# Two forget tables in two PSUM banks, ahead of the values' compression

## The chip, the cores and the metric

The kernel runs on one core of one Trainium2 chip. The metric is the device time of one execution in microseconds (us); lower is better. The kernel is one program of some 22,700 instructions in which the order on every engine is written out by hand and engines meet only at counting semaphores.

## What is computed

The program computes two transformer blocks on 512 tokens of width 1024, in float32. The change lies wholly in the first block, between its input projections and its first attention:

```python
log_f = jax.nn.log_sigmoid(f_f + b_forget).transpose(0, 2, 1)      # (B, H=8, S=512)
# fox_attention
cum = jnp.cumsum(log_f, axis=-1)
s = einsum('bhqd,bhkd->bhqk', qb, k) * scale
s = s + cb[..., :, None] - cum[..., None, :]
s = jnp.where(kpos[None, :] <= qpos[:, None], s, NEG_INF)
p = jax.nn.softmax(s, axis=-1)
# compress_blocks, once for keys (k) and once for values (v)
blk = moveaxis(t[:, idx] + pos, 3, 1).reshape(B, G, n_cmp=31, 32 * 64)
return jax.nn.gelu(blk @ w1) @ w2                                  # w1: 2048 x 256
```

A softmax over keys does not see the query's own sum, so the kernel adds only minus the keys' cumulative sum to the scores. For each of the 8 forgetting ("fox") heads that is a **table** of 128 x 512: the head's row of sums, the same in all 128 partitions.

## The kernel before

**Engines and buffers.** Weights arrive in units of 1 MB (two transfers of 512 KB) by the queue of SP, are split by ScalarE (`split_high(u)`, L419, a rounded high part) and VectorE (`split_low(u)`, L425, the rest), and are used by TensorE as three products per tile (`products`, L434 to L436). There are two raw buffers: `feed(u)` in SP's program waits until `split_low(u - 2)` is done. Units 12 and 13 are the two halves of the keys' compression weight, 14 and 15 those of the values', 16 and 17 the first units of the gates ("ga", AT_MIX = 16).

**TensorE around the change.** After the last projection come, in this order: `compressed(0, 0)` and `compressed(0, 1)` (keys), the cumulative sums (L1143, four matmuls against a triangle of ones into 8 rows of bank 3, `cum_psum`), `compressed(1, 0)` (values, unit 14), `heads_to_features(zk)` (L1096, transposes into banks 4 to 7), `compressed_features(0)` (L1125), `compressed(1, 1)` (unit 15), `compressed_rows(0)` (L1132), and then the attention of the first block, `attend_pe`. It opens with `table(0)` and `table(1)`. `fox_table(g)` (L1164) is one matmul of 8 rows against `cumT`, a row broadcast to 128 partitions, always into bank 7; for g above 0 it first waits until ScalarE has copied table g - 1 (`fox_tab`).

**Attention.** It runs in rounds d of two heads. Round d has: a table where one is due (table 2 in round 0, table 3 in round 1), the transposes of the probabilities of round d - 2 (L568), the scores of two heads (L579) with the causal mask added (L584), and a filling (`fill`) of two weight tiles of the gates, six matmuls. Scores of round d are allowed once VectorE has read those of round d - 1 (`scored`, L640). After the filling of round 0 come `compressed_features(1)` and the transposes L1202, after that of round 1 `compressed_rows(1)`.

**ScalarE around the change.** Its program reads: the tanh of the gates (L1628), `split_high(14)`, GELU of the keys' compression (L1635, with a table load), `split_high(15)`, `split_high(16)`, GELU of the values', a square root (L1521), `split_high(17)`, then the copies of tables 0, 1 and 2 out of bank 7 (L1644), then the first exponentials (L682).

**VectorE around the change.** After `head_norm(3)` (the keys' head norm, four L1957): `split_low(14)`, four small operations on gates and masks (L2018 to L2022), `split_low(15)`, the copy of the cumulative sums `cumT` (L2026, `cum_ready`), `head_copy(3)` (four L1966), `compressed_columns(0)` (L2030), `split_low(16)`, the small norm of the compressed keys (L2037 to L2043, with ScalarE's square root within it), `split_low(17)`, and then round 0 of the attention (L640, twice). The norm's two last operations release TensorE's L1202 (`kcn_ready`).

Of the kernel before, what the change touches and what calls it, by code (L numbers as in the profile page):

```python
# [13 lines left out]
P = 128  # L14
# [177 lines left out]
def build_blocks(nc, w, out):  # L192
# [542 lines left out]
    with block, nc.allow_non_contiguous_dma(reason="gains of heads and outputs, a column each"):  # L735
# [289 lines left out]
        def _(pe):  # L1025
# [102 lines left out]
            def compressed_rows(kv):  # L1128
# [6 lines left out]
                mm.then_inc(s["cmp2_psum"], 1)  # L1135

            pe.wait_ge(s["blk_low"], 1)
            compressed(0, 0)
# [3 lines left out]
            for j in range(NT):  # L1142
                mm = nc.tensor.matmul(ps[3][0:8, :], lf[:, 8 * j:8 * j + 8], upper[:, 384 - P * j:896 - P * j],  # L1143
                                      start=j == 0, stop=j == NT - 1)
            mm.then_inc(s["cum_psum"], 1)
            pe.wait_ge(s["blk_low"], 2)
            compressed(1, 0)
            pe.wait_ge(s["head_ready"], 4)
            heads_to_features(zk, [("blk_ready", 2)] * 2 + [("tr_evac", 12)] * 2)
            compressed_features(0)  # L1150
# [5 lines left out]
            pe.wait_ge(s["gates_ready"], 1)  # L1156
            pe.wait_ge(s["cum_ready"], 1)

            def fox_table(g):
                if g >= H:  # L1160
                    return
                if g:
                    pe.wait_ge(s["fox_tab"], g)
                nc.tensor.matmul(ps[7], view(ident[0:8, :], [[0, P]], g), cumT[0:8, :], start=True, stop=True)\  # L1164
                    .then_inc(s["tab_psum"], 1)

            def fill_chunk(job, c):
# [5 lines left out]
                if c == 0:  # L1173
                    pe.wait_ge(s["split_lo"], u + 1)
                    if kind == "ga" and 1 <= j <= 4:
                        pe.wait_ge(s["gate_scaled"], j)
                    elif kind == "ga" and j == 5:
                        pe.wait_ge(s["fox_tab"], H)
                    elif kind == "ga" and j >= 6:
                        pe.wait_ge(s["gate_scaled"], j - 1)  # L1180
                    elif kind == "fu":
                        pe.wait_ge(s["o_evac"], 4)
                        pe.wait_ge(*((s["gate_scaled"], 7 + j) if j < 2 else (s["mixed"], j - 1)))
                    elif kind == "gb":
                        pe.wait_ge(*((s["mixed"], 7 + j) if j < 2 else (s["gate_scaled"], 8 + j - 1)))
                    elif kind == "nu":
                        pe.wait_ge(s["o_evac"], 8)
                        if j >= 2:
                            pe.wait_ge(*((s["gate_scaled"], 16) if j < 4 else (s["mixed"], 8 + j - 3)))
# [320 lines left out]
        def _(act):  # L1510
# [86 lines left out]
            def z_copy(n, dst, cols):  # L1597
# [30 lines left out]
            nc.scalar.activation(gates.rearrange("p (t n) -> p t n", t=NT), zd[:, :, 256:280], ACT.Tanh, scale=0.5)\  # L1628
                .then_inc(s["gate_raw"], 1)
            for kv in range(2):  # L1630
                split_high(AT_COMPRESS + 2 + kv)
                if kv:
                    split_high(AT_MIX)
# [5 lines left out]
            def fox_table(g):  # L1639
                if g >= H:  # L1640
                    return
                free_tab(act, first, g)
                act.wait_ge(s["tab_psum"], g + 1)
                nc.scalar.activation(tab[:, g % 4, :], ps[7], ACT.Copy).then_inc(s["fox_tab"], 1)  # L1644

# [191 lines left out]
        def _(dve):  # L1837
# [158 lines left out]
            def block_low(kv):  # L1996
# [17 lines left out]
                .then_inc(s["lf_ready"], 1)  # L2014
            head_norm(3)
            split_low(AT_COMPRESS + 2)
            dve.wait_ge(s["gate_raw"], 1)
# [5 lines left out]
            split_low(AT_COMPRESS + 3)  # L2023
            dve.wait_ge(s["cum_psum"], 1)
            dve.wait_ge(s["head_ready"], 4)
            V.tensor_scalar(cumT, ps[3][0:8, :].rearrange("p (t q) -> p t q", t=NT), -1.0, None, ALU.mult).then_inc(s["cum_ready"], 1)  # L2026

# [460 lines left out]
```

## Time and profile before

| | us |
|---|---|
| median of 3 runs | 1940.85 (1937.8 to 1941.66) |
| span of the profiled execution, first to last instruction | 1939.3 |
| TensorE busy in the span | 1823.9 (94%) |
| VectorE busy | 970.1 (50%) |
| ScalarE busy | 863.5 (45%) |
| GpSimd busy | 254.5 (13%) |

The span of the profiled execution lies 1.55 us under the median of the runs; it isn't known which of the three runs, if any, is the profiled one. Most rows below are of the timeline: start, length, engine, line, operation, and in brackets how long the engine was idle before it and what it was then waiting for.

### The profile page before, as it was taken

The page shows a single profiled execution, that of the slowest core. Times are in us where ns is not written, and L with a number is a line of the kernel's source. Part 1 is how long each engine was busy: PE and PEld are TensorE (multiplying, and loading weights), DVE is VectorE, ACT ScalarE, POOL GpSimd, SP SyncE. Part 2 cuts the span into 40 slices and gives each one's busy share as a digit, 9 for nine tenths or more (in the row PEclk, how much of TensorE's full clock was granted, in tenths as well). Part 3 has the DMA queues.
Part 4 walks back from the last instruction along what each step waited for, and adds up shares of the span by engine and source line. Part 5 has one row for each costly group of instructions (what it writes and reads, how often), then busy time and mean ns, then how long its engine had stood idle before and what let it go on. Part 6 is the DMA issues. An engine that isn't in the chain of part 4 may idle for free.

```text
span 1939.3 us, 22676 instructions
## 1 busy us (share of the span) xinstructions
PE 1823.9 (94%) x8553; PEld 1431.7 (74%) x8553; DVE 970.1 (50%) x1549; ACT 863.5 (45%) x1355; POOL 254.5 (13%) x313
## 2 busy tenths in 40 slices
PE   8997999999779999979999999998788999999997
PEld 6885666667668888858888888786554878888886
DVE  4446344445469999964332342625555354423434
ACT  4235665552348888853223231424566143223222
POOL 4000532220001111200000000511223000000000
PEclk9997999999989999999999999998799999999999
DMA  7224011115469999672323332333000133224331
GB/s 208 87 69 130 23 43 46 44 44 190 180 240 373 389 384 382 242 231 66 109 90 94 100 96 98 88 106 98 12 22 23 47 86 96 92 92 109 87 108 54
DMA packets 161283, 246.31 MB, mean 127 GB/s; under 512 B 11586, under 2 KB 117281, under 8 KB 148256
## 3 DMA queue, kind: packets, MB, share of 16 engines
q1 hardware_dynamic: 152880, 232.30, 35.5%
q0 software_dynamic: 8304, 12.69, 2.2%
q8 instruction: 62, 1.02, 0.2%
q14 instruction: 37, 0.30, 0.0%
HBM read 239.15 MB, written 12.61 MB: 130 GB/s over the span
## 4 chain that ended last, share of the span: by engine, by line
PE 86%; DVE 5%; ACT 4%; issue 3%; POOL 1%; DMA 1%; DVEq 0%; SPq 0%; ACTq 0%; POOLq 0%
PE psum L434 25%; PE psum L436 24%; PE psum L435 24%; PE psum L599 3%; PE psum L579 3%; PE psum L568 2%; ACT warea_r L419 1%; PE psum L1269 1%; DVE xarea L1910 1%; POOL arena L699 1%; PE psum L1443 1%; DVE xarea L2280 1%; PE psum L1164 1%; PE psum L1096 0%; DMA arena<-y_assigned 0%
## 5 line engine op out<-in xcount | busy, mean ns | idle before, releaser
L425 DVE TENSOR_TENSOR warea_r<-warea,warea_r 128x2048 fp32r<-128x2048 f32 x110 | 255.3, 2322 | 331.6 <-ACT warea_r L419 331.4
L434 PE MATMUL psum<-tarea_r,warea_r 128*128 128x512 f32 x896 | 357.2, 399 | 3.8 <-DVE tarea_r L1920 3.8
L436 PE MATMUL psum<-tarea_r,warea_r 128*128 128x512 f32 x896 | 351.0, 392 | 0.0
L435 PE MATMUL psum<-tarea_r,warea_r 128*128 128x512 f32 x896 | 350.9, 392 | 0.0
L419 ACT ACTIVATE warea_r<-warea 128x2048 fp32r<-128x2048 f32 x110 | 209.7, 1907 | 271.0 <-PE psum L436 266.1
L434 PE MATMUL psum<-warea_r,arena_r 128*128 128x512 f32 (+1 forms) x768 | 300.4, 391 | 14.0 <-DVE warea_r L425 5.0
L436 PE MATMUL psum<-warea_r,arena_r 128*128 128x512 f32 (+1 forms) x768 | 297.5, 387 | 0.0
L435 PE MATMUL psum<-warea_r,arena_r 128*128 128x512 f32 (+1 forms) x768 | 297.2, 387 | 0.0
L434 PEld LDWEIGHTS psum<-tarea_r,warea_r 128*128 128x128 f32 x896 | 169.2, 189 | 45.0 <-issue 8.4
L436 PEld LDWEIGHTS psum<-tarea_r,warea_r 128*128 128x128 f32 x896 | 169.3, 189 | 36.3
L435 PEld LDWEIGHTS psum<-tarea_r,warea_r 128*128 128x128 f32 x896 | 169.4, 189 | 33.8 <-issue 0.7
L434 PEld LDWEIGHTS psum<-warea_r,arena_r 128*128 128x128 f32 (+1 forms) x768 | 143.7, 187 | 44.4 <-issue 7.4
L436 PEld LDWEIGHTS psum<-warea_r,arena_r 128*128 128x128 f32 (+1 forms) x768 | 143.4, 187 | 29.3
L435 PEld LDWEIGHTS psum<-warea_r,arena_r 128*128 128x128 f32 (+1 forms) x768 | 143.7, 187 | 27.8
L434 PE MATMUL psum<-warea_r,tarea_r 128*128 128x512 f32 (+3 forms) x408 | 157.3, 386 | 1.9 <-DVE tarea_r L2393 1.4
L1751 ACT ACTIVATE arena<-arena 128x512 f32<-128x512 f32 x44 | 27.8, 632 | 294.3 <-DVE arena L2297 294.3
L435 PE MATMUL psum<-warea_r,tarea_r 128*128 128x512 f32 (+3 forms) x408 | 155.6, 381 | 0.0
L436 PE MATMUL psum<-warea_r,tarea_r 128*128 128x512 f32 (+3 forms) x408 | 155.5, 381 | 0.0
L2297 DVE TENSOR_TENSOR arena<-psum,garea 128x512 f32<-128x512 f32 x44 | 30.4, 692 | 178.0 <-PE psum L436 166.2
L903 POOL TENSOR_TENSOR harea<-harea,garea 128x1024 f32<-128x1024 f32 x3 | 7.2, 2385 | 795.7 <-ACT arena L1581 795.7
L579 PE MATMUL psum<-arena 64*128 64x256 f32 (+3 forms) x416 | 87.5, 450 | 2.9 <-DVE nmax L640 2.1
L434 PEld LDWEIGHTS psum<-warea_r,tarea_r 128*128 128x128 f32 x408 | 78.2, 192 | 16.1 <-DVE tarea_r L2393 1.8
(325 smaller groups left out, 2482.6 us busy)
## 6 DMA issues: line engine op xcount, KB each, us to landing
warea<-in_ffn_w_gu SPq DMA_DIRECT2D x88, 512.0 KB, 5.0
warea<-in_w_in SPq DMA_DIRECT2D x40, 512.0 KB, 4.6
warea<-in_ffn_w_down SPq DMA_DIRECT2D x40, 512.0 KB, 4.4
arena<-in_w_up SPq DMA_DIRECT2D x16, 1024.0 KB, 8.1
tarea<-in_w_up SPq DMA_DIRECT2D x16, 1024.0 KB, 7.2
tarea<-in_w_down SPq DMA_DIRECT2D x16, 1024.0 KB, 7.5
warea<-in_w_gate SPq DMA_DIRECT2D x14, 1024.0 KB, 7.7
harea<-in_w_gate SPq DMA_DIRECT2D x14, 1024.0 KB, 7.9
```

The source lines that it names most:

```text
L419: act.activation(w_hi[:, u % 2, :], raw_of(u), ACT.Copy).then_inc(s["split_hi"], 1)
L425: dve.tensor_tensor(w_lo[:, u % 2, :], raw_of(u), w_hi[:, u % 2, :].bitcast(f32), ALU.subtract)\
L434: nc.tensor.matmul(out, high, by_high, start=first, stop=False)
L435: nc.tensor.matmul(out, high, by_low, start=False, stop=False)
L436: return nc.tensor.matmul(out, low, by_high, start=False, stop=last)
L568: mm = nc.tensor.transpose(bank[0:rows, P * j:P * j + P], pbuf[:, c0:c0 + rows], ident)
L579: mm = nc.tensor.matmul(ps[st["e"]][:, a:b], st["lhsT"], rhs, start=True, stop=not (mask and b == n))
L599: mm = nc.tensor.matmul(half(bank, e_)[:, c:d_], lhsT, PT[0:lhsT.shape[0], e_, j, a:b], start=start, stop=stop)
L699: ins = nc.gpsimd.tensor_scalar(p, p, rr[:, k:k + 1], None, ALU.mult)
L1164: nc.tensor.matmul(ps[7], view(ident[0:8, :], [[0, P]], g), cumT[0:8, :], start=True, stop=True)\
L1751: nc.scalar.activation(sgb[:, v % 2, :], sgb[:, v % 2, :], ACT.Silu).then_inc(s["ff_silu"], 1)
L2297: V.tensor_tensor(sgb[:, v % 2, :], ps[2 * (v % 2)], row_of[(2, 4)[g // 2]], ALU.mult).then_inc(s["ff_scaled"], 1)
```

## The change

Tables 0 and 1 are made right behind the cumulative sums, into banks 7 and 6, and are copied by ScalarE between `split_high(14)` and the GELU of the keys' compression. For this VectorE copies the cumulative sums directly behind the keys' head norm, ahead of `split_low(14)`, and TensorE waits for that copy ahead of the tables. TensorE gets a wait for both table copies ahead of `heads_to_features(zk)`, which writes banks 4 to 7, and one ahead of the first gate job, which is in bank 6. Tables 2 to 7 are made as before; table 2 waits for `fox_tab` 2 and table g for `fox_tab` g.

```diff
+            def cum_table(g, bank):
+                nc.tensor.matmul(bank, view(ident[0:8, :], [[0, P]], g), cumT[0:8, :], start=True, stop=True)\
+                    .then_inc(s["tab_psum"], 1)
...
             mm.then_inc(s["cum_psum"], 1)
+            pe.wait_ge(s["cum_ready"], 1)
+            for g in range(2):
+                cum_table(g, ps[7 - g])
             pe.wait_ge(s["blk_low"], 2)
             compressed(1, 0)
             pe.wait_ge(s["head_ready"], 4)
+            pe.wait_ge(s["fox_tab"], 2)
             heads_to_features(zk, [("blk_ready", 2)] * 2 + [("tr_evac", 12)] * 2)
...
-            pe.wait_ge(s["cum_ready"], 1)
 
             def fox_table(g):
-                if g >= H:
+                if g >= H or g < 2:
                     return
-                if g:
-                    pe.wait_ge(s["fox_tab"], g)
-                nc.tensor.matmul(ps[7], view(ident[0:8, :], [[0, P]], g), cumT[0:8, :], start=True, stop=True)\
-                    .then_inc(s["tab_psum"], 1)
+                pe.wait_ge(s["fox_tab"], g)
+                cum_table(g, ps[7])
...
-                    if kind == "ga" and 1 <= j <= 4:
+                    if kind == "ga" and j == 0:
+                        pe.wait_ge(s["fox_tab"], 2)
+                    elif kind == "ga" and 1 <= j <= 4:
...
+            def tables(g, bank):
+                act.wait_ge(s["tab_psum"], g + 1)
+                nc.scalar.activation(tab[:, g % 4, :], bank, ACT.Copy).then_inc(s["fox_tab"], 1)
+
             for kv in range(2):
                 split_high(AT_COMPRESS + 2 + kv)
-                if kv:
+                if kv == 0:
+                    for g in range(2):
+                        tables(g, ps[7 - g])
+                else:
                     split_high(AT_MIX)
...
             head_norm(3)
+            dve.wait_ge(s["cum_psum"], 1)
+            dve.wait_ge(s["head_ready"], 4)
+            V.tensor_scalar(cumT, ps[3][0:8, :].rearrange("p (t q) -> p t q", t=NT), -1.0, None, ALU.mult).then_inc(s["cum_ready"], 1)
             split_low(AT_COMPRESS + 2)
...
             split_low(AT_COMPRESS + 3)
-            dve.wait_ge(s["cum_psum"], 1)
-            dve.wait_ge(s["head_ready"], 4)
-            V.tensor_scalar(cumT, ps[3][0:8, :].rearrange("p (t q) -> p t q", t=NT), -1.0, None, ALU.mult).then_inc(s["cum_ready"], 1)
```

On TensorE the order differs at two places. The first is between the cumulative sums (L1143, in the changed kernel L1147) and the values' compression (62x256); L1138 is a table:

```order
 L435 MATMUL psum<-warea_r,arena_r 62x256
 L436 MATMUL psum<-warea_r,arena_r 62x256
-L1143 MATMUL psum<-const,small 8x512 x4
+L1147 MATMUL psum<-const,small 8x512 x4
+L1138 MATMUL psum<-arena,const 128x512 x2
 L434 MATMUL psum<-warea_r,arena_r 62x256
 L435 MATMUL psum<-warea_r,arena_r 62x256
```

Two tables now stand there. The second is the opening of the attention, between `compressed_rows(0)` (L1132) and the scores of round 0 (L579):

```order
 L436 MATMUL psum<-warea_r,arena_r 62x256
 L1132 MATMUL psum<-arena 31x64 x4
-L1164 MATMUL psum<-arena,const 128x512 x3
+L1138 MATMUL psum<-arena,const 128x512
 L579 MATMUL psum<-arena 128x128 x2
 L584 MATMUL psum<-mask_r 128x128 x2
```

Of three tables in a row one is left, table 2. On ScalarE the rows from the tanh of the gates to the first exponential's table load read, before:

```order
L1628 ACTIVATE small<-arena 128x96
L419 ACTIVATE warea_r<-warea 128x2048
L1635 ACT_TABLE_LOAD
L1635 ACTIVATE arena<-psum 62x256
L419 ACTIVATE warea_r<-warea 128x2048 x2
L1635 ACTIVATE arena<-psum 62x256
L1521 ACT_TABLE_LOAD
L1521 ACTIVATE rstd<-rstd 31x2
L419 ACTIVATE warea_r<-warea 128x2048
L1644 ACTIVATE xarea<-psum 128x512 x3
L682 ACT_TABLE_LOAD
```

and now (L1639 is the table copy, L1649 the GELU, L1528 the square root):

```order
L1635 ACTIVATE small<-arena 128x96
L419 ACTIVATE warea_r<-warea 128x2048
L1639 ACTIVATE xarea<-psum 128x512 x2
L1649 ACT_TABLE_LOAD
L1649 ACTIVATE arena<-psum 62x256
L419 ACTIVATE warea_r<-warea 128x2048 x2
L1649 ACTIVATE arena<-psum 62x256
L1528 ACT_TABLE_LOAD
L1528 ACTIVATE rstd<-rstd 31x2
L419 ACTIVATE warea_r<-warea 128x2048
L1639 ACTIVATE xarea<-psum 128x512
L682 ACT_TABLE_LOAD
```

Two of the three copies stand ahead of the GELU's table load and of three splits. On VectorE one operation moves, the copy of the cumulative sums (L2026). It used to stand behind `split_low(15)`; in the changed kernel it is the operation ahead of `split_low(14)`, as the diff shows.

## Rows read from the trace of the kernel before

**Rows 1.** Page, part 4: the chain that ended last, share by engine.

```profile
PE 86%; DVE 5%; ACT 4%; issue 3%; POOL 1%; DMA 1%; DVEq 0%; SPq 0%; ACTq 0%; POOLq 0%
```

**Rows 2.** Timeline of TensorE, cumulative sums to round 2: start, length, line, [idle<-releaser].

```profile
155.65 3.60 PE L1143 MATMUL psum<-const,small 128*8 128x512 f32 x8
161.90 0.30 PE L434 MATMUL psum<-warea_r,arena_r 128*62 128x256 f32 x1 [2.66 <-DVE warea_r L425]
...
168.37 0.33 PE L434 MATMUL psum<-warea_r,arena_r 128*62 128x256 f32 x1
...
171.90 1.12 PE L1164 MATMUL psum<-arena,const 8*128 8x512 f32 x2
175.67 1.85 PE L1164 MATMUL psum<-arena,const 8*128 8x512 f32 x2 [2.65 <-ACT xarea L1644]
178.21 2.07 PE L1164 MATMUL psum<-arena,const 8*128 8x512 f32 x2 [0.69 <-ACT xarea L1644]
180.21 0.80 PE L579 MATMUL psum<-arena 64*128 64x128 f32 x4
...
186.84 1.23 PE L579 MATMUL psum<-arena 64*128 64x256 f32 x4
...
192.76 0.51 PE L568 MATMUL psum<-const,xarea 128*128 128x128 f32 x2 [0.42 <-issue]
```

**Rows 3.** Timeline of ScalarE, same stretch.

```profile
159.45 1.28 ACT L1635 ACT_TABLE_LOAD   x1
160.74 0.38 ACT L1635 ACTIVATE arena<-psum 62x256 f32<-62x256 f32 x1
...
167.85 1.92 ACT L419 ACTIVATE warea_r<-warea 128x2048 fp32r<-128x2048 f32 x1 [4.93 <-DMA warea<-in_w_in]
171.44 0.38 ACT L1635 ACTIVATE arena<-psum 62x256 f32<-62x256 f32 x1 [1.68 <-PE psum L436]
...
173.25 1.89 ACT L419 ACTIVATE warea_r<-warea 128x2048 fp32r<-128x2048 f32 x1
175.05 0.57 ACT L1644 ACTIVATE xarea<-psum 128x512 f32<-128x512 f32 x1
```

**Rows 4.** Timeline of VectorE, same stretch.

```profile
159.46 2.29 DVE L425 TENSOR_TENSOR warea_r<-warea,warea_r 128x2048 fp32r<-128x2048 f32 x1 [0.61 <-ACT warea_r L419]
...
162.95 2.29 DVE L425 TENSOR_TENSOR warea_r<-warea,warea_r 128x2048 fp32r<-128x2048 f32 x1 [0.55 <-ACT warea_r L419]
165.28 0.68 DVE L2026 TENSOR_SCALAR arena<-psum 8x512 f32<-8x512 f32 x1
166.91 2.73 DVE L1966 TENSOR_SCALAR arena<-psum,small 128x512 f32<-128x512 f32 x4 [0.95 <-PE psum L1096]
...
172.01 0.28 DVE L2037 COPY harea<-psum 31x128 f32<-31x128 f32 x1
...
173.56 0.48 DVE L2043 TENSOR_TENSOR arena<-harea,rstd 31x128 f32<-31x128 f32 x2
175.17 2.29 DVE L425 TENSOR_TENSOR warea_r<-warea,warea_r 128x2048 fp32r<-128x2048 f32 x1 [1.13 <-ACT warea_r L419]
181.60 0.29 DVE L640 CUSTOM_DVE_ANT_0 xarea<-psum,xarea 128x128 f32<-128x128 f32 x1 [4.14 <-PE psum L584]
```

**Rows 5.** Windows: length, busy (instructions) of PE, PEld, DVE, ACT, POOL; PEclk, DMA.

```profile
162.00:166.00 4.00, 4.00 (x22) 4.00 (x23) 3.38 (x5) 0.92 (x1) 0.00 (x0) 0.57 0.80 239
175.00:176.00 1.00, 0.33 (x1) 0.29 (x2) 0.83 (x1) 0.62 (x2) 0.00 (x0) 0.96 1.09 386
192.00:193.00 1.00, 0.58 (x5) 0.37 (x3) 0.28 (x1) 0.00 (x0) 0.00 (x0) 0.50 0.00 0
193.00:440.00 247.00, 237.44 (x1328) 161.08 (x1327) 102.95 (x414) 139.66 (x413) 83.51 (x125) 0.98 0.12 39
```

**Rows 6.** Chain of waits, 140 to 230 us: one table's two passes at full clock.

```profile
203.59 1.05 PE psum L1164 x2
```

**Rows 7.** Waits of SP's own queue, 0 to 300 us: total, times, longest.

```profile
SPq L753 <- DVE warea_r L425: 241.7, 17, 46.6
```

More of the change, by code:

```diff
@@ L1639, in fox_table @@
             def fox_table(g):
-                if g >= H:
+                if g >= H or g < 2:
                     return
                 free_tab(act, first, g)
-                act.wait_ge(s["tab_psum"], g + 1)
-                nc.scalar.activation(tab[:, g % 4, :], ps[7], ACT.Copy).then_inc(s["fox_tab"], 1)
+                tables(g, ps[7])
             def pair_high(ph, dst, gains_=None, squares=None):
```

## The prediction, made before the changed kernel was timed

> **What bounds the kernel now.** I read the chain that ended last first: TensorE holds 86% of it [rows 1], so an edit is worth what it takes off TensorE's line of work, its own time, its waits and the clock at which it works. Then I read TensorE's timeline where the diff touches it. The reader should see two holes. The first, 2.66 us ahead of 161.90, is the wait for the low part of unit 14, the first half of the values' weight [rows 2]. The second is the opening of the attention: table 0 at 171.90, 2.65 us of idling until ScalarE has copied it, table 1 at 175.67, 0.69 us of idling, table 2 at 178.21, and only at 180.21 the first scores [rows 2]. ScalarE's timeline tells why the first copy is late: between the GELU at 171.44 and the copy at 175.05 stand a square root and the split of unit 17, 173.25 to 175.14 [rows 3]. Last I read the clock. It was granted fully until this hole, fell at its end (0.96 in the microsecond from 175) and was at 0.50 up to 193; from 193 to 440 it was 0.98 [rows 5]. An earlier low stretch lies behind the first hole, 0.57 from 162 to 166 [rows 5]. So the hole at the opening costs its idle time, and seems to cost half speed for the 17 us behind it.
>
> The landmark of my sum is the first L568, the transposes of round 2, at 192.76 [rows 2]. Up to it the work of rounds 0 and 1 is the same in both kernels.
>
> **The cumulative sums move forward.** TensorE ends them at 155.65 + 3.60 = 159.25 [rows 2]. VectorE, free since its head norm, now copies them first: 0.68 us [rows 4], 159.25 to 159.93. `split_low(14)` starts at 159.9 instead of 159.46 and ends at 162.2 (+0.44) [rows 4]. SP's transfers wait for just these splits [rows 7], so unit 16 comes 0.44 later as well: its high split can start at 167.85 + 0.44 = 168.3 [rows 3]. Unit 17 is looked at below.
>
> **Two tables at the first hole.** TensorE has nothing to do there. Table 0 can start at about 159.97; a table takes 1.12 us (171.90 row) or 1.05 in a row of matmuls, at full clock [rows 2, 6]. So table 0 ends at 161.1, table 1 at 162.1. The values' compression needs `split_low(14)`; before, it started 0.15 behind that split's end, so now at 162.35 instead of 161.90. The matmuls of the tables cost TensorE nothing, since the split covers them; if the clock were low here (1.85 to 2.07 a table [rows 2]) they would end at 164 and push 1.7 us.
>
> **ScalarE's queue behind the two new waits.** The copies, 0.57 to 0.60 each [rows 3], run 161.1 to 161.7 and 162.1 to 162.7. Behind them wait the GELU's table load (159.45 before, now 162.7), the GELU (now 164.0 to 164.4) and `split_high(15)`, which ran from 161.02 and now runs 164.3 to 166.2: +3.2. TensorE's new wait for both copies ahead of the transposes costs nothing, since these come at 165.3 or later and the copies end at 162.7.
>
> Here the trace speaks against a rule that would charge more. The load took 1.28 us, 159.45 to 160.73, and the GELU began at 160.74 [rows 3]. The Trainium skill, page "ScalarE: Activation LUTs", section "What ACT_TABLE_LOAD costs", counts a drain of about 1.38 us besides the load for every change of set. By the page, an estimate from its figure, ScalarE's chain and with it the gain would be up to 1.4 us worse if the drain showed behind copies. The row shows no gap, and I go by the row.
>
> **The second half of the values' compression.** `split_low(15)` takes 2.29 [rows 4]: 166.2 to 168.5. `compressed(1, 1)` starts at 168.65 instead of 168.37 [rows 2]: +0.28. The 3.2 us on ScalarE are nearly all hidden, since TensorE has the transposes and features between the halves. But VectorE goes in order: `head_copy(3)` takes 2.73 and began at 166.91 [rows 4]; now it begins at 168.45 and ends at 171.2, the columns at 171.4, `split_low(16)` at 171.35 + 2.29 = 173.6 (before 172.1), the norm that began at 172.01 now begins at 173.55: +1.54 on this chain, and `kcn_ready` comes at 174.04 + 1.54 = 175.6.
>
> **The opening of the attention.** TensorE ends `compressed_rows(0)` at about 172.2 (before 171.9). Tables 0 and 1 and both holes are gone; table 2, free to start, runs 172.2 to 173.3. Taken alone this is 178.21 - 172.2 = 6.0 us. At full clock round 0's scores, masks and filling end at about 175.4, the transposes behind `kcn_ready` at 175.85.
>
> What is late next is the ScalarE and VectorE chain. The square root follows the norm (+1.54), `split_high(17)` begins at 173.25 + 1.54 = 174.8 and ends at 176.7. Its transfer is no limit: it is released at 168.5, and the slowest landing near here took 167.85 - 161.75 = 6.1 us [rows 3, 4], so 174.6. The copy of table 2 (0.57) ends at 177.16, table 3 starts at 177.2. `split_low(17)` runs 176.7 to 179.0, and only then VectorE reads the first scores, twice 0.29 with their small reads (181.60 row [rows 4]): done at about 179.5. Round 1's scores wait for that. They stood at 186.84 [rows 2]: 7.3 us earlier. Their tail, 186.84 to 192.76, took 5.9 us at the low clock; at full clock, half of the 5.5 us of work and little waiting, about 3.0.
>
> So L568 comes at 179.5 + 5.9 = 185.4 at the low clock (gain 7.4) or at 182.5 at the full one (gain 10.3).
>
> **The clock.** Between 175.85 and 179.5 TensorE has only table 3 to do (1.1 us). Before, 0.37 + 2.65 us of much the same, table 0 and a hole, stood ahead of the fall at 175 [rows 2, 5]. So I take it that the clock falls again, near 179. It came back before after 17 us which held both holes' rests and three tables [rows 2, 5]; the low stretch of 162 to 166, dense with products, was short [rows 5]. The new stretch holds fewer waits, so I take a return at 186 to 190. Round 2 ran at full clock before; now the low clock's part of it, 1 to 5 us, costs half of that more: gain 7.4 less 0.3 to 2.3, **about 6.3 us**. The Trainium skill, page "TensorE: Matmul & The Clock Gate", section "Why this matters for your kernels", wants no long idle gaps between bursts of matmuls. By it the first gap, now filled with tables, should no longer be followed by half clock; since `split_low(15)` is the bound there, that would alter nothing in the sum.
>
> **Is the gain carried to the end?** From 193 on TensorE is busy 237.4 of 247 us [rows 5], its transfers are released by the splits [rows 7] and not by the time of day, and no engine has work that ends at a fixed time. I carry it in full. The span would be 1939.3 - 6.3 = 1933.0, and with the 1.55 us that lie between span and median, 1934.5.
>
> **Rivals.**
> (a) *The clock does not fall again.* The filling and table 3 suffice. Gain 10.3: 1930.5. Against it: 3.65 us with 1.1 us of work.
> (b) *The clock stays low up to 193, as before.* Gain 7.4 - (193 - 185.4)/2 = 3.6: 1937.2. For it: rounds 0 and 1 were low for the whole of their length.
> (c) *The gain is given back.* Other transfers or engines bound later stages, or the shift moves what TensorE's clock does at later holes; the runs of before alone spread over 3.9 us. Gain 0: 1940.9. Against it: [rows 1, 7].
> (d) *Slower: the low clock carries into the attention.* The new stall ahead of round 1 starts the low stretch at 179 and it lasts twice as long as the old one, 34 us, to 213. It costs half of 213 - 185.4, 13.8 us, less the 7.4 won: 6.4 slower, 1947.3. It decides once the low clock lasts beyond 200, where the gain of 7.4 is used up. Against it: the rounds from 193 on ran at 0.98 [rows 5].
> (e) *The change does not do what it says,* because the first copies come late enough to hold `split_high(15)` much longer. With low clock at the tables (1.7 us more) all that follows comes 1.7 us later and the gain is 4.6: 1936.2.
>
> **How the numbers follow.** Chances: forecast 0.45, (a) 0.22, (b) 0.11, (e) 0.07, (c) 0.11, (d) 0.04. The range leaves out (c) and (d) and little of the spread between runs: 1929.5 to 1938.5. Changes under 0.2% (3.9 us) can't be told from none here. The forecast, (a) and most of (e) are beyond that, (b) just under: faster 0.74, same 0.20, slower 0.06.
>
> **What would show it.** Right: two tables at 160 to 162; `split_high(15)` near 164.3; one table between L1132 and the first scores; no wait of TensorE over 1.5 us between 165 and 180; the first scores near 173.3, those of round 1 near 179.5, waiting for L640; L568 at 184 to 187; a low clock beginning near 179, and the distance of the two traces at 300, 500 and 1500 us the same as at L568. Wrong: a fall of the clock at another place or none; `compressed(1, 1)` more than 1 us later than 168.4; VectorE reading the first scores later than 180.5; or a distance that shrinks behind 440.

## The result

The changed kernel took 1927.54 us (median of 8 runs, 1925.24 to 1935.13), the kernel before, run beside it, 1939.32 us (8 runs). The ratio is 0.9946 with a 95% interval of 0.9931 to 0.9961: some 10 us faster. The forecast was 1934.5 us with a range from 1929.5 to 1938.5. So the sign was right and the forecast gain too small; the time lies 2 us under the range. The profiled execution has a span of 1926.7 us against 1939.3, 12.6 us less. One execution in all the runs below, of the variant fill_before, took 2324.82 us at a granted clock of 0.737 and is left out of that variant's ratio.

The shape of the page is the same; the chain has the shares of [rows 1]:

```profile
PE 86%; DVE 5%; ACT 3%; issue 3%; POOL 1%; DMA 1%; SPq 0%; DVEq 0%; ACTq 0%; POOLq 0%
```

The timeline of TensorE in the changed kernel, from the cumulative sums to round 2 (start, length, engine, line, operation; in brackets idle time and who ended it). It answers [rows 2]:

```profile
155.31 3.60 PE L1147 MATMUL psum<-const,small 128*8 128x512 f32 x8
159.69 1.98 PE L1138 MATMUL psum<-arena,const 8*128 8x512 f32 x4 [0.77 <-DVE arena L2031]
161.97 0.30 PE L434 MATMUL psum<-warea_r,arena_r 128*62 128x256 f32 x1 [0.31 <-DVE warea_r L425]
...
168.26 0.30 PE L434 MATMUL psum<-warea_r,arena_r 128*62 128x256 f32 x1 [1.29 <-DVE warea_r L425]
...
171.77 1.12 PE L1138 MATMUL psum<-arena,const 8*128 8x512 f32 x2
172.82 0.49 PE L579 MATMUL psum<-arena 64*128 64x128 f32 x4
...
176.72 1.12 PE L1138 MATMUL psum<-arena,const 8*128 8x512 f32 x2 [1.12 <-ACT xarea L1639]
179.00 1.22 PE L579 MATMUL psum<-arena 64*128 64x256 f32 x4 [1.15 <-DVE nmax L640]
...
184.91 0.41 PE L568 MATMUL psum<-const,xarea 128*128 128x128 f32 x2 [0.42 <-issue]
```

The two tables sit in the first hole, one table is left at the opening, the first scores come at 172.8 instead of 180.2 and L568 of round 2 at 184.9 instead of 192.8. ScalarE and VectorE, against [rows 3, 4]:

```profile
160.84 0.60 ACT L1639 ACTIVATE xarea<-psum 128x512 f32<-128x512 f32 x1 [3.17 <-PE psum L1138]
161.70 0.60 ACT L1639 ACTIVATE xarea<-psum 128x512 f32<-128x512 f32 x1 [0.26 <-PE psum L1138]
162.31 1.28 ACT L1649 ACT_TABLE_LOAD   x1
163.61 0.38 ACT L1649 ACTIVATE arena<-psum 62x256 f32<-62x256 f32 x1
163.89 1.90 ACT L419 ACTIVATE warea_r<-warea 128x2048 fp32r<-128x2048 f32 x1
...
174.30 1.90 ACT L419 ACTIVATE warea_r<-warea 128x2048 fp32r<-128x2048 f32 x1
```

```profile
165.83 2.29 DVE L425 TENSOR_TENSOR warea_r<-warea,warea_r 128x2048 fp32r<-128x2048 f32 x1 [3.35 <-ACT warea_r L419]
...
176.23 2.29 DVE L425 TENSOR_TENSOR warea_r<-warea,warea_r 128x2048 fp32r<-128x2048 f32 x1 [1.13 <-ACT warea_r L419]
178.44 0.28 DVE L640 CUSTOM_DVE_ANT_0 xarea<-psum,xarea 128x128 f32<-128x128 f32 x1
```

The split of unit 15 on ScalarE starts at 163.89, not 161.0, and pushes VectorE's splits. The windows of one microsecond (busy per engine, then PEclk, DMA share, GB/s) show where the clock fell and came back, against [rows 5] (1.00 is the full clock and 0.50 the low level; a value between them means that the window has both):

```profile
177.00:178.00 1.00, 0.84 (x2) 0.01 (x1) 1.00 (x1) 0.97 (x1) 0.00 (x0) 1.00 0.69 240
178.00:179.00 1.00, 0.01 (x1) 0.01 (x1) 0.94 (x5) 0.24 (x1) 0.00 (x0) 0.52 0.00 0
...
184.00:185.00 1.00, 0.58 (x6) 0.37 (x5) 0.28 (x1) 0.00 (x0) 0.00 (x0) 0.57 0.00 0
185.00:186.00 1.00, 1.00 (x10) 0.71 (x10) 0.00 (x0) 0.45 (x2) 0.00 (x0) 1.00 0.00 0
```

It fell at 178.0 and was back at 184.9: 6.9 us low instead of 17. Before, it had fallen at 175.9 and come back at 193.0.

**Where the other microseconds came from.** I set the start of the same matmul in several traces against the first trace of before (it is counted from the end of the program; for dense_after, which has added matmuls, from the start in the first two columns). The changed kernel's first trace, the two later ones of each kernel (below) and two variants, in us:

| start in the first trace of before | 100 | 156 | 193 | 300 | 430 | 560 | 1235 | 1270 | 1500 | 1560 |
|---|---|---|---|---|---|---|---|---|---|---|
| before_again | -1.8 | -0.3 | -1.1 | -1.2 | -1.2 | -1.2 | -1.6 | -3.2 | 0.0 | -2.2 |
| before_3 | -0.8 | -0.8 | -1.0 | -1.0 | -1.0 | +1.2 | +2.5 | +2.5 | +5.2 | +1.8 |
| after | -1.8 | -0.3 | -8.0 | -7.9 | -7.9 | -8.1 | -8.2 | -9.8 | -10.4 | -12.6 |
| after_again | -1.8 | -0.2 | -9.8 | -9.9 | -4.4 | -4.5 | -4.3 | -4.3 | -4.4 | -4.4 |
| after_3 | -2.0 | -1.9 | -9.3 | -9.3 | -9.3 | -9.3 | -9.5 | -11.1 | -11.6 | -13.8 |
| split17_late | -0.8 | -0.8 | -13.4 | -11.8 | -11.7 | -9.2 | -8.8 | -10.5 | -12.0 | -12.1 |
| dense_after | 0.0 | 0.0 | -8.8 | -8.8 | -6.2 | -3.8 | -3.7 | -5.3 | -5.7 | -7.8 |

Between 156 and 193 the changed kernel wins 7.6 us in its first trace; the distance then stands still up to 1235. The rest of the 12.6 is 0.3 in front of 156 and 4.4 in steps behind 1235, at about 1240 and between 1300 and 1560, in code that is the same in both. Are these part of the change, or chance? This was the first question for the chip.

### The profile page after: what moved, and what is told of

Read it like the earlier page. It is cut to its first block, busy times and chain, and to the rows that moved or that the text cites. A ratio compares the mean times of both kernels' runs of the same rounds, so it can differ in the third digit from the quotient of the medians.

```text
span 1926.7 us, 22677 instructions
## 1 busy us (share of the span) xinstructions
PE 1813.8 (94%) x8553; PEld 1425.6 (74%) x8553; DVE 969.3 (50%) x1549; ACT 863.5 (45%) x1355; POOL 255.7 (13%) x313
## 4 chain that ended last, share of the span: by engine, by line
PE 86%; DVE 5%; ACT 3%; issue 3%; POOL 1%; DMA 1%; SPq 0%; DVEq 0%; ACTq 0%; POOLq 0%
PE psum L434 25%; PE psum L436 24%; PE psum L435 24%; PE psum L579 3%; PE psum L599 3%; PE psum L568 2%; ACT warea_r L419 1%; PE psum L1276 1%; DVE xarea L1923 1%; POOL arena L699 1%; DVE xarea L2293 1%; PE psum L1450 0%; DMA xarea<-in_x 0%; DMA arena<-y_assigned 0%; POOL xarea L699 0%
## 5 line engine op out<-in xcount | busy, mean ns | idle before, releaser
L579 PE MATMUL psum<-arena 64*128 64x256 f32 (+3 forms) x416 | 88.3, 453 | 3.7 <-DVE nmax L640 2.8
```

The source lines that it names most:

```text
L579: mm = nc.tensor.matmul(ps[st["e"]][:, a:b], st["lhsT"], rhs, start=True, stop=not (mask and b == n))
```

## Experiments

In what follows "the distance" is the time from the start of the cumulative sums to L568 of round 2. It leaves out what an execution wins or loses before them. "Half clock" is the part of the distance in which the granted clock was 0.50. The last two columns say how far the trace moved against the first trace of before between 193 and 1235 us and between 1235 and 1560 us of that trace (minus is a gain).

| kernel | cumulative sums start | scores of round 0, 1 | L568 of round 2 | distance | half clock | 193 to 1235 | 1235 to 1560 |
|---|---|---|---|---|---|---|---|
| before | 155.65 | 180.21, 186.84 | 192.76 | 37.1 | 20.3 | 0.0 | 0.0 |
| before_again | 155.33 | 179.18, 185.80 | 191.72 | 36.4 | 20.5 | -0.4 | -0.7 |
| before_3 | 154.83 | 179.35, 185.98 | 191.84 | 37.0 | 20.5 | +3.5 | -0.6 |
| after | 155.31 | 172.82, 179.00 | 184.91 | 29.6 | 6.8 | -0.3 | -4.4 |
| after_again | 155.42 | 174.34, 179.53 | 183.04 | 27.6 | 6.8 | +5.5 | -0.1 |
| after_3 | 153.71 | 171.34, 177.51 | 183.43 | 29.7 | 10.0 | -0.2 | -4.3 |
| fill_before | 154.80 | 178.48, 185.11 | 191.03 | 36.2 | 13.6 | +0.8 | -0.7 |
| dense_before | 155.55 | 178.92, 184.11 | 187.61 | 32.1 | 6.8 | -1.1 | +1.3 |
| b_split17_late | 156.86 | 179.12, 184.46 | 187.93 | 31.1 | 10.2 | +2.1 | -0.3 |
| split_first | 155.25 | 171.75, 178.54 | 184.47 | 29.2 | 6.6 | -0.2 | -4.8 |
| one_table | 155.57 | 178.09, 183.54 | 187.02 | 31.5 | 10.2 | -1.7 | -4.4 |
| one_bank | 155.63 | 175.51, 180.84 | 184.33 | 28.7 | 6.8 | +1.3 | -4.1 |
| dense_after | 155.61 | 174.56, 180.57 | 184.05 | 28.4 | 3.4 | +5.1 | -4.1 |
| split17_late | 154.84 | 172.34, 176.03 | 179.50 | 24.7 | 0.0 | +4.5 | -3.2 |

### Both kernels again: is the rest of the gain chance?

Nothing is edited: these are further traces of each kernel.

> The kernel before, once more, for a second draw of TensorE's clock. Theory 1 (the part of the gain that the rounds 0 and 1 don't explain is chance: where the low-clock stretches fall at the start, near 1244 us and in the second block's attention differs from execution to execution): against the first trace of before, this one differs by up to 2 us at the start, near 1244 and between 1340 and 1520, with steps of the size seen between before and after (1.75, 1.6, 2.8 us). Theory 2 (these steps belong to the shift that the change makes): this trace lies within 0.3 us of the first one of before at every landmark.

> The changed kernel, once more. Both theories: L568 of round 2 near 185 against 193 and a ratio of 0.993 to 0.996. Theory 1: the distance to a trace of before in front of the change (at 140 us) and behind 1240 us is not again -1.75 and -4.6, but anything from -3 to +3. Theory 2: both come again within 0.5 us.

> A third trace of the kernel before. Theory 1 (outside rounds 0 and 1 the clock differs by chance): L568 of round 2 is 36 to 37.5 us behind the cumulative sums again; at least one step of more than 1 us against the other two traces of before shows at the start or behind 200.

> A third trace of the changed kernel. Theory 1: L568 of round 2 is 27.5 to 31 us behind the cumulative sums; the 4.6 us that the first trace won at the start and behind 1240 don't come back as such, the distances there lie anywhere from -5 to +3.

Measured: the steps up to 1235 are not the change's. The kernel before against itself moved by 1.8 us in the first 20 us, by 1.6 at 1240, by 3.2 us between 1270 and 1500 (before_again) and by 6.2 between 430 and 1500 (before_3). The second trace of the changed kernel has won none of the first one's 4.4 us behind 1235 and has lost 5.4 us between 300 and 430. The windows show the clock behind it. 10 to 20 us, in the first trace of before, then in before_again:

```profile
10.00:20.00 10.00, 8.17 (x30) 6.43 (x31) 7.56 (x9) 8.02 (x10) 7.21 (x14) 0.66 0.67 233
```

```profile
10.00:20.00 10.00, 8.34 (x38) 7.30 (x39) 7.65 (x9) 7.55 (x10) 7.32 (x14) 1.00 0.70 246
```

And 300 to 440 us, in the first trace of after and in after_again:

```profile
300.00:440.00 140.00, 132.36 (x718) 91.66 (x717) 57.70 (x227) 72.55 (x221) 36.67 (x68) 0.96 0.16 55
```

```profile
300.00:440.00 140.00, 132.36 (x701) 91.15 (x700) 56.14 (x223) 72.35 (x219) 35.76 (x67) 0.93 0.13 44
```

The granted clock of the same code differs between executions. The distance, on the other hand, comes again: 36.4 to 37.1 before, 27.6 to 29.7 after. The mean gain up to L568 is 36.84 - 28.98 = 7.9 us. The half clock within the distance comes again too: about 20 us in each trace of before, 7 to 10 in those of the changed kernel. Its place does not. In after it lies from 178.0 to 184.9, in after_again from 161.2 to 168.0 and nowhere behind the opening, in after_3 from 159.8 to 163.2 and from 176.9 to 183.7. Half of the difference in low time, an estimate that takes TensorE for busy throughout it, is 6.3 of the 7.9 us. That leaves 1.6 for the holes and the tables themselves.

Theory 1 holds for before_again, before_3 and, behind 1240, for after_again (whose -1.8 at the start is again that of after), but not for all that after_3 was to show: its distances at the start (-2.0) and behind 1235 (-4.3) are nearly those of the first trace of after (-1.8 and -4.4). The last column of the table shows more. Between 1235 and 1560 seven of the eight traces with early tables gain 3.2 to 4.8 us; the eighth is after_again. None of the six traces of the kernel before and its variants (the first is the measure) gains more than 0.7. One of these steps can be named: the low stretch at 1244 of before (1244.3 to 1247.7) is in five of those six and in one of the eight. So the gain behind 1235 goes with the change in most executions. Why it does, in code that is the same, these traces don't show.

The second comparison in time: after_again 1929.6 us (9 runs), ratio 0.9955 (0.9934 to 0.9975). Over all comparisons the kernel before was run 70 times, median 1938.6 (1937.9 to 1940.8 in the four comparisons), and the changed one 18 times, median 1928.9: 9.7 us. The traces show 7.9 of these up to L568. The other 1.8 are what the three traces of each kernel give from 193 to 1560 as well, by their means (-1.2 against +0.6), but this hangs on single losses such as the 5.4 us of after_again; how much of it would come again is open.

### Filling the holes of the kernel before: how much is the clock?

In `fox_table` of the kernel before:

```diff
+                if g in (1, 2):
+                    keep_busy(ps[6], 3 if g == 1 else 1)
                 if g:
                     pe.wait_ge(s["fox_tab"], g)
```

> The kernel before with idle matmuls in the two holes of the attention's opening (three behind table 0, one behind table 1, 0.9 us each), into a free bank; everything else is as before, the wait for the copies too. Theory C (most of the gain of rounds 0 and 1 is the clock: the holes let it fall to 0.50 for 17 us): it stays at 1.00 and L568 of round 2 comes near 185.5 to 187, 6 to 7 us earlier, ratio 0.996 to 0.997. Theory H (the gain is the removed holes and tables, the clock falls anyway): L568 stays within 1 us of 192.8, ratio 1.000.

Measured: ratio 0.9991 (0.9971 to 1.0011), distance 36.2. Theory C failed as I put it; the distance stayed within 1 us, as theory H has it. The filling ran, and the clock fell nevertheless, as TensorE's timeline and two windows of fill_before show:

```profile
170.56 2.84 PE L1030 MATMUL psum<-const 128*128 128x512 f32 x6
174.84 1.12 PE L1166 MATMUL psum<-arena,const 8*128 8x512 f32 x2 [1.43 <-ACT xarea L1646]
175.89 1.13 PE L1030 MATMUL psum<-const 128*128 128x512 f32 x2
176.94 1.61 PE L1166 MATMUL psum<-arena,const 8*128 8x512 f32 x2
```

```profile
177.00:178.00 1.00, 1.00 (x3) 0.23 (x2) 0.00 (x0) 0.00 (x0) 0.00 (x0) 0.72 0.30 29
...
190.00:191.00 1.00, 0.61 (x6) 0.37 (x5) 0.28 (x1) 0.00 (x0) 0.00 (x0) 0.50 0.00 0
```

TensorE was busy from 174.84 on, without a gap, and was set to half speed at 177.4, up to 191.1. The hole of 1.43 us that was left had ended 2.6 us earlier; in the first trace of before the fall came 0.2 us behind the end of one of 2.65 us. So a hole right ahead of it is not needed for the fall. The next kernel fills with another kind of matmul:

```diff
+            def dense(bank, n):
+                for _ in range(n):
+                    nc.tensor.matmul(bank, hT_hi[:, 0, 0:P], hT_hi[:, 0, :], start=True, stop=True)
...
+                if g in (1, 2):
+                    dense(ps[6], 11 if g == 1 else 3)
```

> The kernel before with the holes of the opening filled by matmuls of the weights' kind (128x512 in the products' number format, 11 behind table 0 and 3 behind table 1, 0.23 us each at full clock). The float32 filling of the run before this one kept TensorE busy for all but 1.4 us of the 6 us ahead of 177.4 and the clock fell all the same. Theory C2 (the clock falls here because tables and float32 matmuls don't hold it, products do): no stretch at 0.50 begins between 171 and 185, and L568 of round 2 comes 35.5 to 31 us behind the start of the cumulative sums (37.1 in the kernel before, 29.6 in the changed one). Theory H (the clock has no part in it): it falls again and L568 is 36 to 37.5 us behind.

Measured: distance 32.1, 5.0 us less than in the first trace of before, though all tables, copies and waits are as they were. Windows of dense_before:

```profile
172.00:179.00 7.00, 6.72 (x22) 3.23 (x21) 4.18 (x9) 4.12 (x5) 0.00 (x0) 1.00 0.51 153
179.00:183.00 4.00, 4.00 (x15) 2.77 (x16) 0.67 (x5) 2.76 (x6) 0.61 (x1) 0.57 0.81 257
183.00:190.00 7.00, 6.58 (x41) 4.30 (x41) 2.64 (x13) 2.38 (x8) 1.63 (x3) 1.00 0.00 0
```

A low stretch is left, but it starts at 179.3 and lasts 3.4 us instead of 17, so the first half of what I expected of C2 (none before 185) failed and the second (31 to 35.5) held. What the 17 us cost the kernel before is 5.0 us by this pair, and near 6.7 with the last 3.4 us (half of them) added, an estimate. The time was 1936.06 us, a single run, from which nothing follows.

### One part of the change, and one bank

One table only, against the changed kernel:

```diff
-            for g in range(2):
-                cum_table(g, ps[7 - g])
+            cum_table(0, ps[7])
...
-            pe.wait_ge(s["fox_tab"], 2)
+            pe.wait_ge(s["fox_tab"], 1)
             heads_to_features(zk, ...)
...
-                if g >= H or g < 2:
+                if g >= H or g < 1:
...
-                    for g in range(2):
-                        tables(g, ps[7 - g])
+                    tables(0, ps[7])
```

> The changed kernel with only table 0 made ahead of the values' compression; tables 1 and 2 at the opening as before, in bank 7. Theory (what counts is that no copy stands between split 17 and the first scores): table 1 is copied behind split 17, at 176, table 2 waits for it, and most of the gain is lost: L568 of round 2 33 to 36 us behind the start of the cumulative sums (37.1 before, 29.6 changed). Rival (each table removed from the opening is worth its own share, half): 33.3 or less, with the first scores before 176.

Measured: the first scores come 22.5 us behind the start of the cumulative sums, 1.3 to 2.0 us earlier than in the three traces of before and 5 us later than in after, as the theory has it; table 2 waits for table 1's copy behind the split of unit 17:

```profile
171.98 1.12 PE L1138 MATMUL psum<-arena,const 8*128 8x512 f32 x2
176.09 2.07 PE L1138 MATMUL psum<-arena,const 8*128 8x512 f32 x2 [2.99 <-ACT xarea L1638]
178.09 0.80 PE L579 MATMUL psum<-arena 64*128 64x128 f32 x4
```

But the distance was 31.5, under the 33 to 36 expected and within what the rival gave, because this execution's low stretch ended at 182.1, after 6.8 us. Against after_3, which has as much half clock in its distance (10.0 us against 10.2), one table fewer costs 1.8 us. So the holes are cured only by both tables; the length of the low stretch goes its own way: with a hole of 2.65 to 2.99 us at the opening it was 17.1 us in before, 10.2 in b_split17_late (below) and 6.8 here. What sets the length is not shown. The time, a single run, was 1929.21 us.

Both early tables in one bank, against the changed kernel:

```diff
             for g in range(2):
-                cum_table(g, ps[7 - g])
+                if g:
+                    pe.wait_ge(s["fox_tab"], g)
+                cum_table(g, ps[7])
...
-                        tables(g, ps[7 - g])
+                        tables(g, ps[7])
```

> The changed kernel with both early tables in bank 7, table 1 behind the copy of table 0. Theory (the ScalarE chain behind the copies carries a delay to the opening in full): second copy 0.6 to 0.9 us later, split of unit 15 and compressed(1, 1) as much later, first scores read 0.5 to 0.9 us later (relative to the start of the cumulative sums). Rival (two banks matter for more): the compression's first half is pushed by over 1 us as well.

Measured: table 1 starts 0.69 us behind table 0's end and took 1.71 us, since the clock had fallen at 162.2. The trace to set beside it is after_again, where the clock was low over nearly the same stretch (161.2 to 168.0 there, 162.2 to 169.0 here) and not again behind the opening. Behind the cumulative sums' start the second copy comes at 7.9 us instead of 6.8, the compression at 7.8 instead of 6.7, the scores of round 1 at 25.2 instead of 24.1, L568 at 28.7 instead of 27.6. Each is 1.1 us later: the delay at the copies goes through to the opening in full, which was the theory, but it is above the 0.6 to 0.9 that I gave, and the compression's push of 1.1 us is the rival's. The second bank is thus worth 1.1 us by this pair, one trace of each. Against the first trace of after the same kernel is 0.9 us ahead; where the low stretch falls can hide the bank's price. The time, a single run, was 1929.77 us.

### What bounds the changed kernel's opening

In ScalarE's program, against the changed kernel:

```diff
+            split_high(AT_COMPRESS + 2)
+            split_high(AT_COMPRESS + 3)
             for kv in range(2):
-                split_high(AT_COMPRESS + 2 + kv)
                 if kv == 0:
```

> The changed kernel with ScalarE's high split of unit 15 moved ahead of the two table copies, into the 3.17 us in which ScalarE waits for table 0. If the new bound of the opening is the chain GELU, split of unit 15, VectorE's low split, head copies (the prediction's step), compressed(1, 1) starts 1.3 us earlier (near 167), and the first read of the scores 2 us earlier (176.5 instead of 178.4); L568 of round 2 at 182 to 183.5, 1.5 to 3 us before the changed kernel's, ratio to the kernel before 0.992 to 0.994. If it isn't the bound, L568 stays at 185.

Measured: `compressed(1, 1)` starts at 166.84 instead of 168.26, as expected, but the distance is 29.2, 0.4 less than in after, and not 1.5 to 3. ScalarE in split_first:

```profile
163.54 0.38 ACT L1650 ACTIVATE arena<-psum 62x256 f32<-62x256 f32 x1
168.47 1.91 ACT L419 ACTIVATE warea_r<-warea 128x2048 fp32r<-128x2048 f32 x1 [4.54 <-DMA warea<-in_w_in]
```

The transfer of unit 16 takes over. It lands at 168.47, and the low split, the small norm, the root and the split of unit 17 all stand behind it. The step of the prediction that the queue behind the copies is what makes the opening late was thus right by 0.4 us only; a second limit lies right under it. The time (1933.69 us, ratio 0.9976, 0.9958 to 0.9993) is even above the changed kernel's, 4.8 us over the median of its 18 runs. The profiled execution was one of the variant's fastest (1927.79), so no trace shows where the others lost time; this stays open.

Now the split of unit 17, on the kernel before (b_split17_late) and on the changed one (split17_late):

```diff
+    split_at[1] = [AT_MIX + 1]
...
-            split_high(AT_MIX + 1)
...
-            split_low(AT_MIX + 1)
```

> The kernel before, with its three tables where they were, but the split of unit 17 moved on both engines from ahead of the attention to the end of round 1. Theory: it is this split that the first table copy waits for; without it the copy of table 0 comes at 173.4 instead of 175.05, VectorE reads the first scores right behind them, L568 of round 2 comes 1.7 us (holes alone) to 5 us (with a shorter low clock) earlier, 32 to 35.4 us behind the start of the cumulative sums, ratio 0.997 to 0.999. Rival: the tables in one bank bound it anyway and it stays within 1 us of 37.1.

> The changed kernel with the split of unit 17 moved on both engines to the end of round 1. Theory (the new bound of the opening is the chain split of unit 17, copy of table 2, VectorE's low split, first scores read): the two holes of 1.12 and 1.15 us ahead of table 3 and of round 1's scores are gone or under 0.3 us, the scores of round 1 start near 176.5 instead of 179.0, the clock need not fall, L568 of round 2 is 24 to 27.5 us behind the start of the cumulative sums instead of 29.6; ratio to the kernel before 0.992 to 0.995, 1 to 4 us under the changed kernel. If the transfer of unit 16 or the small norm bounds it, the gain is under 1 us.

Measured on the kernel before: copy 0 starts at 173.74, 11.9 us behind the start of `compressed(1, 0)` instead of 13.2. It is now the square root ahead of it that sets it (173.63, after a wait of 1.79 for the norm). The hole ahead of table 1 is 2.65 us, as it was; the tables in one bank keep the first scores at 179.1. So both holes of the kernel before stay when only the split moves. The low stretch lasted 10 us, and the distance was 31.1, a little under the 32 to 35.4 expected. Ratio 0.9991 (0.9973 to 1.001): I can't tell the time from that of before.

On the changed kernel the same three lines do what was expected. TensorE in split17_late:

```profile
175.00 1.10 PE L1139 MATMUL psum<-arena,const 8*128 8x512 f32 x2
176.03 0.70 PE L579 MATMUL psum<-arena 64*128 64x256 f32 x4
...
179.50 0.41 PE L568 MATMUL psum<-const,xarea 128*128 128x128 f32 x2 [0.42 <-issue]
...
184.43 0.41 PE L568 MATMUL psum<-const,xarea 128*128 128x128 f32 x2 [1.65 <-POOL xarea L699]
```

```profile
150.00:200.00 50.00, 43.69 (x258) 28.51 (x259) 29.79 (x71) 32.87 (x61) 10.76 (x11) 1.00 0.34 106
```

Both holes are gone, the clock is full from 150 to 200, the distance is 24.7, 4.9 us less than after's. The new bound is seen too: GpSimd's scaling, which TensorE waits for at 184.43, for 1.65 us. Of the 5 us not much is left at the end. The table of the starts shows -13.4 at 193, -11.8 at 300 and -9.2 at 560. The first of these losses, 1.6 us, sits exactly at that wait for GpSimd. The kernel before with the split moved has the same wait (1.66 us) and loses the same there, so it is the price of the moved split. The losses between 430 and 560 are steps of the clock. The time was 1927.54 us (6 runs), ratio 0.9939 (0.9919 to 0.9958), the lowest ratio of all, but not to be told from the changed kernel's.

The last kernel puts the matmuls of dense_before (the function `dense`) into the changed kernel's holes and into banks that are free: behind the cumulative sums, ahead of `compressed(1, 1)` and around table 3.

```diff
+            dense(ps[7], 3)
             pe.wait_ge(s["cum_ready"], 1)
...
+            dense(ps[0], 5)
             compressed(1, 1)
...
+                if g == 3:
+                    dense(ps[4], 4)
                 pe.wait_ge(s["fox_tab"], g)
                 cum_table(g, ps[7])
+                if g == 3:
+                    dense(ps[4], 4)
```

> The changed kernel with idle matmuls of the products' format in its own holes (3 behind the cumulative sums, 5 ahead of compressed(1, 1), 4 ahead of table 3 and 4 behind it). Theory (the low clock behind 178 is worth 3.4 us of the 29.6 and comes from these holes): no stretch at 0.50 begins between 156 and 185, L568 of round 2 is 26 to 27.5 us behind the start of the cumulative sums, ratio to the kernel before 0.992 to 0.995. Rival (holding the clock here only moves a low stretch into the attention): L568 comes early, but at 300 us the distance to the changed kernel is under 1 us.

Measured: the low stretch behind 178 is gone, one from 162.3 to 165.8 is there (as in the first trace of before), so none between 156 and 185 was wrong; the distance is 28.4, above the 26 to 27.5 expected. Windows of dense_after:

```profile
162.00:166.00 4.00, 3.74 (x20) 3.76 (x20) 0.74 (x5) 3.92 (x4) 0.00 (x0) 0.57 0.72 205
166.00:200.00 34.00, 33.50 (x194) 22.77 (x194) 18.60 (x54) 19.30 (x44) 10.67 (x11) 1.00 0.33 100
300.00:560.00 260.00, 233.34 (x1151) 172.31 (x1149) 115.97 (x335) 109.64 (x268) 41.17 (x73) 0.91 0.32 120
```

At 300 the start is 0.9 us ahead of after's, a distance under 1 us as the rival said, and by 560 it is 4.3 us behind it, at a clock of 0.91 between 300 and 560. That the filling moved a low stretch there, which is the rival's reason, is not shown: after_again, without any filling, has low stretches at the same places (294 to 301 and 342 to 349 us; 295 to 302 and 343 to 347 here). The ratio is 0.9973 (0.9955 to 0.9991). The gain is about half of the smallest expected (0.995), and the median of 1932.25 us is 3.4 above that of the changed kernel. The idle matmuls pay nothing in time.

## Why the prediction was wrong

The path, the waits and the holes came out as forecast. The step that failed is the sizing of what stands around them: the return of the clock, the base time, and the stages behind 193 us, in which the prediction let nothing change.

- **The two tables at the first hole, at no cost for TensorE:** right. It gave 159.97 to 162.1, and 162.35 for the compression; with this execution's earlier start of 0.34 us that is what the rows have (159.69 to 161.67, 161.97).
- **ScalarE's queue:** right within 0.1 us, the load at 1.28 us without a gap behind it (162.31 to 163.59, GELU at 163.61). The drain that the Trainium skill, page "ScalarE: Activation LUTs", section "What ACT_TABLE_LOAD costs", counts besides the load does not show behind table copies either.
- **The opening:** scores of round 1 forecast at 179.5, measured 179.0; both waits named (ScalarE's copy of table 2, VectorE's read of the scores) are there with 1.12 and 1.15 us. The forecast of L568 was 185.4, measured 184.91.
- **The clock:** a fall near 179 forecast, 178.0 measured. (The prediction likened it to "0.37 + 2.65 us" ahead of the old fall. The 0.37 is in no row of that timeline: table 0 alone took 1.12.) The return was the first term that was mis-sized: 186 to 190 forecast, 184.9 measured. The 0.3 to 2.3 us that I took off round 2 for it weren't there. The three traces of the changed kernel give 7.9 us on average up to L568, against the 6.3 forecast: 1.6 us. That the fall near 179 comes at all was right in two of the three traces only. The first hole, now filled with tables, was followed by half clock in those of after_again (161.2) and after_3 (159.8) and not in that of after.
- **The base:** the second term. I set the span's gain against 1940.85, the median of three runs. Over 70 runs the median is 1938.6, so 2.2 us of the distance to the measured time were no gain at all. The three runs' own spread of 3.9 us could have told me that the base was uncertain by much of the 5.0 us between the forecast and the range's lower end.
- **Carried in full:** right as far as 1235 in two traces: the first keeps its -8, the third its -9.3. It failed otherwise. The prediction wanted the same distance at 300, 500 and 1500 as at L568. The second trace shrank from -9.9 at 300 to -4.4 at 430, and behind 1235 the first and the third won 4.4 and 4.3 us more.
- **The rest:** 9.7 us by the medians against 7.9 by the traces, 1.8 that the prediction put at nothing. Together the three make up the distance from the forecast to the changed kernel's median over 18 runs: 1.6 + 2.2 + 1.8 = 5.6, and 1934.5 - 1928.9 = 5.6. The first two are shown. The third is the balance of losses behind 193 and gains behind 1235. The gains go with the early tables in seven of eight traces; their cause stays open. The eight runs of the result lie another 1.3 us lower, at 1927.54; the nine of the second comparison lie at 1929.6.
- **Rivals:** (a) was right in after_again, where the clock did not fall behind the opening; but it fell earlier, from 161.2 to 168.0. (b) and (d) are out. So is (e): in after_again and after_3 the clock did fall at the early tables, and the gain up to 193 was still over 7 us. (c), a gain given back, holds for part of one trace, after_again. That the steps of the clock add several us either way I had only within (c), as a loss. I did not widen the range downward for them, and with the base 2.2 us too high this is why 1927.5 fell outside.

## What to carry to other kernels

When an engine waits for a small copy at the opening of a phase, look at what is queued ahead of that copy on its engine: here a weight split not needed for another eight rounds stood before it. Moving the split alone left both holes of the opening; moving the tables took these out and left two of 1.1 us; moving both left none there, at the price of a new wait of 1.65 us for GpSimd one round later. Behind each limit that such an edit removes sat another within half a microsecond to two (transfer of unit 16, small norm, GpSimd's scaling), so follow the chain for one more step before setting the price. Where TensorE's clock moves between its two levels, compare the start of the same instruction along both traces, and that of one kernel with itself; this tells in one view where the edit moved the work. To tell the edit from the clock, set beside each other those traces that have equal time at half clock in the stretch in question.

## What I had not expected of the hardware

- TensorE's granted clock fell to 0.50 at 177.4 in fill_before while the engine had been busy without a gap since 174.84, with float32 matmuls of 128x512 and with tables of 8 rows. The page "TensorE: Matmul & The Clock Gate" of the Trainium skill, section "Why this matters for your kernels", advises to avoid idle gaps; the trace has no gap in those last 2.6 us, only one of 1.43 us ahead of them, so gaps alone do not tell the story. With matmuls in the products' format in the same holes, the full clock held to 179.3. That the kind of matmul is the cause rests on one trace of each and is not shown.
- The same kernel has some of its low stretches at other places in each execution: 12 to 19 us, 151 to 154 us and 162 to 166 us are there in some traces and not in others, and the loss between 300 and 430 us was 0 in two executions of the changed kernel and 5.4 us in a third. Others go with the kernel more than chance would have it: the stretch at 1244 us is in five of six traces with the tables at the opening and in one of eight with early tables. For the kernel before, 70 runs lie between 1930.8 and 1948.1 us. The median of the three runs from which the prediction started lay 2.2 us, or 0.12%, above the median of the 70.
